# Normalising the attention probabilities on GpSimd instead of spreading the reciprocals with a product, in the first mixer

## The reference, cut to what matters

```
def one_block(args):
    qn, kn, vn, mn = args
    s_loc = where(mn, einsum('bqhgd,bkhd->bhgqk', qn, kn), NEG_INF)
    s_ctx = einsum('bqhgd,bchd->bhgqc', qn, kc)
    p = softmax(concatenate([s_sink, s_ctx, s_loc], axis=-1), axis=-1)
    return (einsum('bhgqc,bchd->bqhgd', p_ctx, vc) + einsum('bhgqk,bkhd->bqhgd', p_loc, vn))
b_l = _windowed_attention(q_l, k_l, v_l, k_cx, v_cx, attn_sink) * silu(b_gate)
```

## Time and profile before

| | before |
|---|---|
| median of 3 runs | 3554.87 us (3551.2 to 3555.83) |
| the profiled execution, its own time | 3556.01 us |
| its span | 3554.2 us |
| TensorE busy | 3395.0 us, 96% |
| VectorE busy | 2138.8 us, 60% |
| GpSimd busy | 2020.2 us, 57% |
| ScalarE busy | 1097.0 us, 31% |
| attention of layer 0, turn(0) to the last weigh | 141.2 us |
| attention of layer 1, the same | 117.3 us |

### The profile page before, as it was taken

One profiled execution on the slowest core, in us unless ns is written; L12 is line 12 of the kernel. 1 busy time (PEld: TensorE's weight loads), 2 busy tenths in 40 slices (PEclk: granted clock), 3 DMA queues, 4 the chain that ended last, 5 costly groups with the idle time before them and its releaser, 6 DMA issues.

```text
span 3554.2 us, 52243 instructions
## 1 busy us (share of the span) xinstructions
PE 3395.0 (96%) x19872; PEld 2721.4 (77%) x19872; DVE 2138.8 (60%) x3077; ACT 1097.0 (31%) x1803; POOL 2020.2 (57%) x2230
## 2 busy tenths in 40 slices
PE   5999999999999999999899999998999979999997
PEld 3887788878778767887678888876787768888885
DVE  5684834559672466335676666664544576666666
ACT  4114633221453332233322222233223232222222
POOL 3342013667203478448867767766646876677774
PEclk9999999999999999999999999999999989999998
DMA  5510011331001243223211111113312311111112
GB/s 216 219 54 13 2 32 38 118 119 54 19 4 42 76 166 99 60 63 125 80 54 54 54 54 54 54 66 107 95 54 84 131 43 59 54 54 54 54 36 77
DMA packets 96777, 256.63 MB, mean 72 GB/s; under 512 B 8592, under 2 KB 34192, under 8 KB 95760
## 3 DMA queue, kind: packets, MB, share of 16 engines
q1 hardware_dynamic: 80048, 215.53, 17.7%
q10 hardware_dynamic: 16480, 37.76, 3.6%
HBM read 228.09 MB, written 16.78 MB: 69 GB/s over the span
## 4 chain that ended last, share of the span: by engine, by line
PE 82%; DVE 8%; POOL 5%; ACT 2%; issue 2%; DMA 1%; SPq 0%; DVEq 0%; ACTq 0%; POOLq 0%
PE banks L827 11%; PE banks L829 11%; PE banks L828 11%; PE banks L1381 7%; PE banks L1380 7%; PE banks L1379 7%; PE banks L1419 4%; PE banks L1421 4%; PE banks L1420 4%; POOL w_lo L2939 4%; PE banks L962 2%; PE banks L976 2%; PE banks L995 2%; DVE nt L2231 1%; POOL w_hi L2936 1%
## 5 line engine op out<-in xcount | busy, mean ns | idle before, releaser
L827 PE MATMUL banks<-h_hi,w_hi 128*128 128x512 f32 (+1 forms) x2160 | 841.4, 390 | 27.6 <-POOLq L2944 26.4
L829 PE MATMUL banks<-h_hi,w_lo 128*128 128x512 f32 (+1 forms) x2160 | 820.9, 380 | 0.0
L828 PE MATMUL banks<-h_lo,w_hi 128*128 128x512 f32 (+1 forms) x2160 | 817.4, 378 | 0.0
L2936 POOL CAST w_hi<-raw 128x1024 fp32r<-128x1024 f32 x198 | 231.8, 1171 | 983.1 <-PE banks L829 555.9
L2939 POOL TENSOR_TENSOR w_lo<-raw,w_hi 128x256 fp32r<-128x256 f32 x792 | 752.6, 981 | 15.9
L827 PEld LDWEIGHTS banks<-h_hi,w_hi 128*128 128x128 f32 x2160 | 408.6, 189 | 124.8 <-POOLq L2944 38.0
L828 PEld LDWEIGHTS banks<-h_lo,w_hi 128*128 128x128 f32 x2160 | 408.7, 189 | 84.5 <-issue 7.7
L829 PEld LDWEIGHTS banks<-h_hi,w_lo 128*128 128x128 f32 x2160 | 407.9, 189 | 78.3
L1419 PE MATMUL banks<-g_slot,w_hi 128*128 128x512 f32 x704 | 281.0, 399 | 10.4 <-DVE g_slot L2823 7.3
L1421 PE MATMUL banks<-g_slot,w_lo 128*128 128x512 f32 x704 | 278.7, 396 | 0.0
L1420 PE MATMUL banks<-g_slot,w_hi 128*128 128x512 f32 x704 | 277.6, 394 | 0.0
(11 more groups left out here) (299 smaller groups left out, 5984.1 us busy)
## 6 DMA issues: line engine op xcount, KB each, us to landing
raw<-w_in SPq DMA_DIRECT2D x118, 512.0 KB, 3.3
raw<-w_out SPq DMA_DIRECT2D x64, 512.0 KB, 3.3
pair_y<-w_ffn SPq DMA_DIRECT2D x20, 1024.0 KB, 5.0
raw<-w_ffn SPq DMA_DIRECT2D x20, 1024.0 KB, 4.9
x<-w_mod SPq DMA_DIRECT2D x16, 1024.0 KB, 6.9
wk<-residual ACTq DMA_DIRECT2D x42, 256.0 KB, 2.9
piece<-w_down SPq DMA_DIRECT2D x40, 256.0 KB, 2.9
nt<-w_down SPq DMA_DIRECT2D x40, 256.0 KB, 2.8
```

The lines of the kernel that those rows point to most:

```text
L827: mm(o, wh[:, ws], hi[:, kt, t0:t0 + n], start=kt == 0, stop=False)
L828: mm(o, wh[:, ws], lo[:, kt, t0:t0 + n], start=False, stop=False)
L829: last = mm(o, wl[:, ws], hi[:, kt, t0:t0 + n], start=False, stop=kt == nk - 1)
L2936: link(G.tensor_copy(w_hi[:, sl], raw[:, sl]))
```

## The change

- `inverse` takes both reciprocals in one instruction, which waits for both exponentials.
- GpSimd gets a new step `normalise(i)`: in place, each head's exponentials times its reciprocal, one `tensor_scalar` for each head; the second raises `norm_ready`. It stands in GpSimd's stream between the split of `lr` and that of `cq`, for all pairs.
- `turn(i)` waits for `norm_ready` instead of for the exponentials.
- `weigh` has no product that spreads the reciprocals, and `mix` no multiplication by them.
- `masked` forms both shifts in one instruction behind both maxima. `scores` and both exponentials wait for that.
- Two semaphores of the convolution become one, with the same order of events.

```
                 def scores(i):
-                        pe.wait_ge(sem["nmax_ready"], 2 * s)
+                        pe.wait_ge(sem["nmax_ready"], s)
                 def turn(i):
-                    pe.wait_ge(sem["exp_ready"], 2 * s + 2)
+                    pe.wait_ge(sem["norm_ready"], s + 1)
                 def weigh(i):
-                    pe.wait_ge(sem["rec_ready"], 2 * s + 2)
-                    for g in range(2):
-                        c = 8 * (s % 4) + 6 + g
-                        mm(psum[7][g * HD:(g + 1) * HD, (2 + s % 2) * P:(3 + s % 2) * P], at_col[:, c:c + 1].broadcast_to([P, HD]), ident,
-                           start=True, stop=True)
                 def exponential(i, g):
-                    act.wait_ge(sem["nmax_ready"], 2 * s + g + 1)
+                    act.wait_ge(sem["nmax_ready"], s + 1)
                 def masked(i):
                     for g in range(2):
-                        link(V.tensor_tensor_reduce(..., at_col[:, c + g:c + g + 1]))
-                        V.tensor_scalar(at_col[:, c + 2 + g:c + 3 + g], at_col[:, c + g:c + g + 1], -HD ** -0.5, nsink[:, h + 4 * g:h + 4 * g + 1],
-                                        ALU.mult, ALU.min).then_inc(sem["nmax_ready"], 1)
+                        last = V.tensor_tensor_reduce(..., at_col[:, c + g:c + g + 1])
+                    link(last)
+                    V.scalar_tensor_tensor(at_col[:, c + 2:c + 4], at_col[:, c:c + 2], -HD ** -0.5, nsink[:, h:h + 5:4],
+                                           ALU.mult, ALU.min).then_inc(sem["nmax_ready"], 1)
                 def inverse(i):
-                    for g in range(2):
-                        dve.wait_ge(sem["exp_ready"], 2 * s + g + 1)
-                        V.reciprocal(at_col[:, c + 6 + g:c + 7 + g], at_col[:, c + 4 + g:c + 5 + g]).then_inc(sem["rec_ready"], 1)
+                    dve.wait_ge(sem["exp_ready"], 2 * s + 2)
+                    V.reciprocal(at_col[:, c + 6:c + 8], at_col[:, c + 4:c + 6]).then_inc(sem["rec_ready"], 1)
                 def mix(i):
-                    link(V.tensor_tensor(m, psum[7][:, (s % 2) * P:(s % 2 + 1) * P], m, ALU.mult))
-                    V.tensor_tensor(m, psum[7][:, (2 + s % 2) * P:(3 + s % 2) * P], m, ALU.mult).then_inc(sem["mixa_ready"], 1)
+                    V.tensor_tensor(m, psum[7][:, (s % 2) * P:(s % 2 + 1) * P], m, ALU.mult).then_inc(sem["mixa_ready"], 1)
                 # GpSimd, behind split_through(lr) and ahead of split_through(cv1)
+                def normalise(i):
+                    s, (j, n) = PAIR0[l] + i, pairs[i]
+                    w, c = len(keys_of(n)) * P, 8 * (s % 4) + 6
+                    pool.wait_ge(sem["rec_ready"], s + 1)
+                    for g in range(2):
+                        p = at_p[i % 3][:, g, 2:2 + w]
+                        last = G.tensor_scalar(p, p, at_col[:, c + g:c + g + 1], None, ALU.mult)
+                    last.then_inc(sem["norm_ready"], 1)
+                for i in range(len(pairs)):
+                    normalise(i)
```

More of the change, by code:

```diff
@@ L459, in two_mixers @@
         act_step dve_step pool_step
-        glu_ready u_ready conv_ready moment_ready cent_ready csq_ready csd_ready cn_ready csilu_ready
+        glu_ready u_ready conv_ready moment_ready cent_ready cstat_ready cn_ready csilu_ready
         gate_ready mixc_ready
         raw_ready rot_ready cosm_ready rope_ready vt_ready vn_ready vz_ready
-        sc_ready nmax_ready exp_ready rec_ready pt_ready pta_copied ptd_copied o_ready mixa_ready
+        sc_ready nmax_ready exp_ready rec_ready norm_ready pt_ready pta_copied ptd_copied o_ready mixa_ready
         z_ready zabs_ready la_ready turned v_copied kt_copied cum_ready ex_ready dec_ready dec_spread kd_ready kin_ready
@@ L941, in _ @@
                 for j in range(2):
-                    pe.wait_ge(sem["csq_ready"], 2 * l + j + 1)
+                    pe.wait_ge(sem["cstat_ready"], 3 * l + j + 1)
                     for ci, (t0, w) in enumerate(chunks):
@@ L1000, in _ @@
                 pe.wait_ge(sem["rope_ready"], 5 * l + 1)
-                pe.wait_ge(sem["csd_ready"], l + 1)
+                pe.wait_ge(sem["cstat_ready"], 3 * (l + 1))
                 bg3 = proj_index(l, "bg3")
@@ L1623, in _ @@
                 for j in range(2):
-                    A(cv_sq[j][:, 0:end], cv_a[j][:, 0:end], ACT.Square).then_inc(sem["csq_ready"], 1)
+                    A(cv_sq[j][:, 0:end], cv_a[j][:, 0:end], ACT.Square).then_inc(sem["cstat_ready"], 1)
                 raw_query(1)
@@ L1630, in _ @@
                 link(last)
-                A(cv_rs[:, 0:end], cv_rs[:, 0:end], ACT.Exp, scale=-0.5).then_inc(sem["csd_ready"], 1)
+                A(cv_rs[:, 0:end], cv_rs[:, 0:end], ACT.Exp, scale=-0.5).then_inc(sem["cstat_ready"], 1)
                 for j in range(2):
@@ L2355, in _ @@
                 rope(1, at_q[0])
-                dve.wait_ge(sem["csd_ready"], l + 1)
+                dve.wait_ge(sem["cstat_ready"], 3 * (l + 1))
                 for j in range(2):
@@ L2379, in masked @@
                     for g in range(2):
-                        link(V.tensor_tensor_reduce(at_s[s % 2][:, g, 2:2 + w], banks[:, 1024 * g + 256:1024 * g + 256 + w], mask_of(n),
-                                                    1.0, -3e38, ALU.add, ALU.max, at_col[:, c + g:c + g + 1]))
-                        V.tensor_scalar(at_col[:, c + 2 + g:c + 3 + g], at_col[:, c + g:c + g + 1], -HD ** -0.5, nsink[:, h + 4 * g:h + 4 * g + 1],
-                                        ALU.mult, ALU.min).then_inc(sem["nmax_ready"], 1)
+                        last = V.tensor_tensor_reduce(at_s[s % 2][:, g, 2:2 + w], banks[:, 1024 * g + 256:1024 * g + 256 + w], mask_of(n),
+                                                      1.0, -3e38, ALU.add, ALU.max, at_col[:, c + g:c + g + 1])
+                    link(last)
+                    V.scalar_tensor_tensor(at_col[:, c + 2:c + 4], at_col[:, c:c + 2], -HD ** -0.5, nsink[:, h:h + 5:4],
+                                           ALU.mult, ALU.min).then_inc(sem["nmax_ready"], 1)
                 def inverse(i):
@@ L2979, in _ @@
                 split_through(proj_index(l, "lr"))
+                pairs = PAIRS[l]
+                def normalise(i):
[8 more added lines that the diff above has]
+                    normalise(i)
                 split_through(proj_index(l, "cv1"))
```

## The result

The changed kernel takes 3621.89 us (median of 4 runs, 3618.69 to 3623.55) against 3555.01 us before: a ratio of 1.0192, 95% interval 1.0178 to 1.0205, so 1.9% slower, 66.9 us. I had forecast 3541 us with a range up to 3578. The prediction is wrong in size and in sign; what happened is its rival B, the mechanism of a turn that waits for GpSimd, at a price above even that rival's.

What follows compares the result with a forecast made beforehand. TensorE, busy 96% of the span, bounds the kernel; relieved, attention turns meet loops through GpSimd and ScalarE. Gains of 6.4 (layer 0), 7.0 (layer 1) and 1.4 us (stage ends) sum to -14.8: 3541 us, range 3535 to 3578.

Steps and rivals of the forecast that it cites:

- rival B: Attention loop: GpSimd's operation costs the price of two tensors, about 1.6 us, so turn waits; +37 us, 3592; chance 0.23.
- d: Time of one GpSimd normalise operation on 640 columns, taken as 0.80 us; the whole change nets zero at 1.04 us.
- bound "from above": Upper price of GpSimd's operation on 640 columns, interpolated from rows that read two tensors: 1.63 us.
- my own formula: Attention loop through GpSimd: F is 2.15 + 2d us, and half of F's growth counts in some 62 turns.
- F: Attention loop: time from the end of scores to the turn they release through other engines; 3.75 us through GpSimd.
- The order on VectorE: Attention loop: reciprocal of pair i + 2 stands behind masking of pair i + 3, so turn waits for GpSimd.
- the closed form (F + W)/2: Average loop turn when F exceeds W, TensorE's work per turn; 3.57 us for layer 0's first turn.
- the gain of 14.8 us: Both attention stages: 6.4 us in layer 0, 7.0 in layer 1, 1.4 at the stage ends.
- the joined shift as something that is covered: ScalarE's loop: joining delays exp by 0.84 us, covered by a pair of 3.98 us, no longer by 3.61.
- the splits behind the stage: Split of cq moved behind the last normalise: 3.8 us, covered by over 10 us, so put at nothing.
- The work behind the stages is of its old length: Expected sign after the attention stages: the rest of the kernel takes as long as before.
- my own upper bound (3592): Kernel time under rival B, 37 us slower; the stated range ended at 3578, leaving out that rival's upper half.

Runs made afterwards that it cites:

- run 4: Changed kernel with GpSimd's tensor_scalar taking a constant (1/32) instead of the reciprocals, leaving the division by the sums out: 3623.98 us in one run.
- run 8: Changed kernel with one GpSimd tensor_tensor for both heads in place of two tensor_scalar: 3556.04 us, ratio 1.0005 to the kernel before.
- run 7: Changed kernel with two 128x256 filler products per loop turn on TensorE before its wait for GpSimd: 3607.42 us, ratio 1.0147 to the kernel before.
- run 3: Changed kernel with GpSimd copying each head's exponentials onto themselves instead of multiplying, division left out: 3537.31 us in one run.
- run 1: Kernel before with only the shifts joined and the reciprocals joined, spread product kept, no GpSimd step: 3554.08 us, ratio 0.9997.
- run 5: Changed kernel with GpSimd multiplying only the first half of each head's columns: 3550.30 us, ratio 0.9986 to the kernel before.
- run 2: Changed kernel without GpSimd's normalise, division left out, turn waiting for the exponentials: 3534.58 us, ratio 0.9942 to the kernel before.
- run 11: Changed kernel with one GpSimd tensor_tensor for both heads, reciprocals ahead of the masking, and shifts apart: 3539.66 us, ratio 0.9961 to the kernel before.
- both remedies: Changed kernel with one GpSimd tensor_tensor for both heads and VectorE's reciprocals ahead of the masking: 3618.43 us, ratio 1.0181 to the kernel before.

## Why the prediction was wrong

**The price of GpSimd's operation: the step that failed.** "What d is the trace does not show ... The operation reads one tensor, so I take a value near the lower end and add a little for the scalar: 0.80 us." It was 1.88 us. The number of tensors read was the wrong thing to compare by: a tensor_scalar with one input costs 1.81 us even with a constant (run 4), a tensor_tensor with two inputs 1.16 us for the same 640 elements (half of 2.32, run 8). Even the bound "from above" of 1.63 us, from two-tensor rows, was no bound, and there the reading was at fault: I took four quick operations of 256 columns and the quicker group of 1024. The view of the earlier trace rows also has, in the kernel before:

```profile
L2939 POOL TENSOR_TENSOR w_lo<-raw,w_hi 128x256 fp32r<-128x256 f32 x792 | 752.6, 981 | 15.9
...
L3025 POOL TENSOR_TENSOR wk<-wk,x 128x1024 f32<-128x1024 f32 x8 | 24.4, 3054 | 1.6 <-POOL w_lo L2939 1.3 <-POOL wk L3019 0.4
```

Between these two, 640 columns come to 0.98 + 384/768 x 2.07 = 2.02 us, a bound that would have held 1.88. With 1.88 put into my own formula: F = 5.91, (5.91 - 3.75)/2 = 1.08 a turn above the forecast, 62 x 1.08 = 67, less 14.8, is +52 us. The tiles that ran at a clock of 1.00 give 4 x 6.1 + 4 x 6.4 = 50 us.

**The clock: a step that was missing.** No rival had a term for it; I took it from the 1.00 of both stages that it would stay there. It did not, with TensorE idle for a fifth of the stage. It cost about 20 us in the stages, and filling the idle time won back 14.5 us net (run 7). The 69.5 us of the stages, 50 at full clock and about 20 by the lower one, with +4.5 ahead of and between them and -7.6 behind, make the 66.5 us by which the profiled spans differ. (52 from the formula and 14.5 from run 7 make 66.5 too, but that is luck: the cost of run 7's own products is in neither, nor are the +4.5 and -7.6.)

**What held.** The order on VectorE as the reason for the wait; the closed form (F + W)/2; the gain of 14.8 us if GpSimd is quick (17 with d = 0.72; run 3 has 14.9 in the stages and 16 in all); the joined shift as something that is covered (run 1); the splits behind the stage, which cost at most the 2.9 us by which the stretch between the stages grew. The work on rival B had the right place and said "it decides from d = 1.04 on"; run 5 puts this near 1.06 in the stages and near 1.15 for the whole kernel. What the forecast put at nothing and was not: "The work behind the stages is of its old length"; it took 7.6 us less, which is hidden in the 66.9. I gave B and its kind 0.23 and the forecast 0.55 on one unmeasured price that alone decided the sign, and drew the range short of my own upper bound (3592).

The rule of the Trainium skill that I weighed (GPSIMD Engine Reference, section 3.1, 1.8 cycles an element as the best of a tight loop) would have given 1.15 us; section 4.1, one-input work "roughly line-rate", gave about my price. Measured is 2.5 ns, 3.0 cycles at the 1.2 GHz of that page: neither gives the price of tensor_scalar here, while the copy is at the line rate ((0.720 - 0.400)/384 = 0.83 ns an element, 1.0 cycle).

**Left open.** From the end of layer 1's stage to the end of the kernel the changed kernel takes 2483.1 us, the one before 2490.7. The kernels without the spread product lie at 2480 to 2487 there, the two with it at 2491 and 2494, each in one profiled execution. The differences sit in several stretches of 2 to 6 us. The granted clock of the first 186 us behind the stage does not sort them: it is 0.97 before and 0.99 without the division, but 0.97 with the copies too, which gain as much. I have no experiment that ties them to the product. It also means that the 20 us of run 2, the sign of run 5 and some 6 of the 13.9 us of run 11 are not the stages' own.

## What to carry to other kernels

An operation that the trace does not hold has no price yet: where it alone decides the sign, the range must reach over rows of every kind on that engine and over the dearest of each kind (2.02 us here, where 1.63 was too low), and the one-line experiment comes first; between a copy, a tensor_scalar and a tensor_tensor on GpSimd the price differed by a factor of 2.6 here. Moving work to an idle engine is free only if the loop has room for its whole length: ask behind which instruction its input stands in the stream ahead of it, since changing that order alone was worth 40 us here, and a cheaper operation alone 66. An engine that idles in short waits can lose clock as well: the 20 us were in no term. And a small operation of VectorE with two SBUF inputs on the path, beside a long tensor_tensor of GpSimd, undid both remedies; look for small operations that end with GpSimd's. Last, a whole kernel's time can agree with a sum for the wrong reason: compare the stretch that the sum is about.

## What the hardware showed that I had not expected

- GpSimd, 128x640 float32 in place: copy 0.72 us, tensor_scalar by a constant 1.81 us, by an operand for each partition 1.88 us; tensor_tensor with a broadcast operand 2.32 us for 128x1280.
- A 128x2 scalar_tensor_tensor of VectorE took 0.85 us instead of 0.16 beside GpSimd's tensor_tensor, and ended with it to 0.02 us, in 63 of 63 cases; beside GpSimd's tensor_scalar it took 0.16 us in 60 of 63. Two 128x1 tensor_scalar operations inside the same tensor_tensor took their usual 0.21 us; a 128x2 one in run 8 took 0.84.
- Products whose results nobody reads made a kernel 14.5 us faster, with TensorE's granted clock at 1.00 in both stages, where it had been 0.91 and 0.96.
